# Causal attention in a two-block fp32 kernel: values as the stationary operand, two heads in two column halves, and the inverse sums turned by TensorE

## The reference, cut to what matters

```python
def one_block(args):                      # Q_BLOCK = 128 queries
    q_blk, blk_idx = args
    s = jnp.einsum('bhqd,bhkd->bhqk', q_blk, k).astype(jnp.float32) * scale
    query_pos = blk_idx * Q_BLOCK + jnp.arange(Q_BLOCK)
    s = jnp.where(key_pos[None, :] <= query_pos[:, None], s, NEG_INF)
    p = jax.nn.softmax(s, axis=-1).astype(v.dtype)
    return jnp.einsum('bhqk,bhkd->bhqd', p, v)
...
o = o.transpose(0, 2, 1, 3).reshape(bsz, seq, N_HEADS * V_DIM)
x = x + o @ mla_w_o[j]
```

## Time and profile before

| | |
|---|---|
| median of 3 runs | 1814.56 us (1811.64 to 1814.99) |
| the profiled execution | 1814.82 us, its span 1813.0 us |
| TensorE matmuls busy | 1755.1 us, 97% |
| VectorE / ScalarE / GpSimd busy | 817.3 / 665.4 / 705.8 us |
| mean granted clock of TensorE | 0.985 of full speed |

### The profile page before, as it was taken

How to read it: one execution, slowest core, us unless ns; L and a number is a source line. 1 busy time by engine, 2 the same in 40 slices (tenths; PEclk the granted TensorE clock), 3 DMA queues, 4 the chain that set the end, 5 groups by cost and what they waited for, 6 DMA issues and landing times.

```text
span 1813.0 us, 22687 instructions
## 1 busy us (share of the span) xinstructions
PE 1755.1 (97%) x9006; PEld 1459.8 (81%) x9006; DVE 817.3 (45%) x1398; ACT 665.4 (37%) x1128; POOL 705.8 (39%) x331
## 2 busy tenths in 40 slices
PE   8999999999999887999999999999999999999999
PEld 6887877787788676789888888888888888888887
DVE  4876999679866536414211111147665311111111
ACT  3332334143243555524322322266755333122221
POOL 5422334435444222243453444424711244344442
PEclk9999999999999898899999999999999999999999
DMA  9422324443535447322333233222200333332332
GB/s 243 100 70 82 86 78 143 124 140 117 167 109 165 134 158 239 105 93 82 100 98 93 88 105 99 81 82 74 75 1 13 93 94 93 94 104 85 101 95 80
DMA packets 242280, 189.61 MB, mean 105 GB/s; under 512 B 41472, under 2 KB 199296, under 8 KB 242176
## 3 DMA queue, kind: packets, MB, share of 16 engines
q1 hardware_dynamic: 238176, 180.33, 33.3%
q10 hardware_dynamic: 4000, 7.84, 1.3%
HBM read 168.74 MB, written 19.40 MB: 104 GB/s over the span
## 4 chain that ended last, share of the span: by engine, by line
PE 82%; DVE 11%; ACT 4%; issue 2%; DMA 1%; ACTq 1%; POOL 0%; DVEq 0%; SPq 0%
PE ps L371 12%; PE ps L373 12%; PE ps L372 12%; PE ps L397 9%; PE ps L398 9%; PE ps L399 9%; PE ps L428 3%; PE ps L429 3%; PE ps L430 3%; PE ps L881 2%; PE ps L862 2%; PE ps L872 1%; ACT w_hi L1147 1%; DVE x_rows L1669 1%; PE ps L854 1%
## 5 line engine op out<-in xcount | busy, mean ns | idle before, releaser
L1020 POOL TENSOR_TENSOR w_lo<-w_raw,w_hi 128x1024 fp32r<-128x1024 f32 (+3 forms) x283 | 668.6, 2373 | 1033.0 <-ACT w_hi L1147 1033.0
L371 PE MATMUL ps<-a_hi,w_hi 128*128 128x512 f32 (+1 forms) x1184 | 442.4, 374 | 4.3 <-POOL w_lo L1020 4.3
L373 PE MATMUL ps<-a_hi,w_lo 128*128 128x512 f32 (+1 forms) x1184 | 440.4, 372 | 0.0
L372 PE MATMUL ps<-a_lo,w_hi 128*128 128x512 f32 (+1 forms) x1184 | 440.3, 372 | 0.0
L1147 ACT ACTIVATE w_hi<-w_raw 128x1024 fp32r<-128x1024 f32 (+3 forms) x283 | 284.9, 1018 | 213.1 <-DMA w_raw<-in_ffn_w_gate_up_dram 70.9
L371 PEld LDWEIGHTS ps<-a_hi,w_hi 128*128 128x128 f32 x1184 | 223.0, 188 | 45.4 <-issue 7.2
L373 PEld LDWEIGHTS ps<-a_hi,w_lo 128*128 128x128 f32 x1184 | 223.0, 188 | 38.9
L372 PEld LDWEIGHTS ps<-a_lo,w_hi 128*128 128x128 f32 x1184 | 223.1, 188 | 38.1
L2134 DVE TENSOR_TENSOR ev<-ps,xh 128x512 f32<-128x512 f32 x44 | 30.4, 692 | 411.9 <-PE ps L373 383.0
L397 PE MATMUL ps<-w_hi,h_hi 128*128 128x512 f32 x476 | 190.7, 401 | 7.2 <-DVE x_rows L1641 3.4
L398 PE MATMUL ps<-w_lo,h_hi 128*128 128x512 f32 x476 | 189.5, 398 | 0.0
(11 more groups left out here) (346 smaller groups left out, 2395.6 us busy)
## 6 DMA issues: line engine op xcount, KB each, us to landing
w_raw<-in_ffn_w_gate_up_dram SPq DMA_DIRECT2D x88, 512.0 KB, 3.8
w_raw<-in_w_up_dram SPq DMA_DIRECT2D x44, 512.0 KB, 3.8
w_raw<-in_ffn_w_down_dram SPq DMA_DIRECT2D x40, 512.0 KB, 3.6
w_raw<-in_w_in_dram SPq DMA_DIRECT2D x20, 512.0 KB, 4.3
w_raw<-in_w_down_dram SPq DMA_DIRECT2D x20, 512.0 KB, 4.2
s_records<-stage SPq DMA_DIRECT2D x16, 544.0 KB, 5.3
w_raw<-in_ssm_w_glu_dram SPq DMA_DIRECT2D x16, 512.0 KB, 3.6
rec<-s_records SPq DMA_DIRECT2D x12, 544.0 KB, 3.7
```

The lines of the kernel that those rows point to most:

```text
L371: pe.matmul(bank, wh, xh_, start=first, stop=False)
L372: pe.matmul(bank, wh, xl_, start=False, stop=False)
L373: return pe.matmul(bank, wl, xh_, start=False, stop=last)
L1020: pool.tensor_tensor(w_lo[:, n % RING, 0:w], w_raw[:, n % RING, 0:w], w_hi[:, n % RING, 0:w].bitcast(F), ALU.subtract).then_inc(lo_made, 1)
```

## The change

- The values become the stationary operand (64 columns), the turned probabilities move. Tile layout: `p_ts` holds two heads, so that for key block j all queries from block j on lie in one row of 512, 384, 256 or 128 numbers.
- `head_out` goes; `pair_out(n)` makes the output of heads 2n and 2n + 1, one in partitions 0 to 63 and one in 64 to 127 of one bank, the heads alternating. The output comes out turned, with queries along the row. It is issued in the even loop turns from h = 2 on, behind the scores of t = 1; that of the last pair lies inside the first product with `mla_w_o_2`.
- The inverse sums are wanted as a row of the same layout. VectorE takes the reciprocal of the 8 columns of sums of a pair, each repeated 64 times (`inverse_sums`, output 128 x 512), in odd loop turns behind `masked(h + 1, 0)`. TensorE waits for it (`sum_inverse`) and turns it with 4 transposes (`inverses`), ScalarE copies it to `inv_rows`, VectorE multiplies the pair's output by it in PSUM (`pair_scaled`), and ScalarE and VectorE split the product into `a_hi` and `a_lo`.
- `head_turn(h + 2)` moves from the end of the loop turn to t = 1.
- `turn_rows("o_t", ...)` and its wait go.

```diff
-            def head_out(h):
-                b = open_bank(("o", h))
+            def inverses(n):
+
+                pe.wait_ge(sum_inverse, n + 1)
+                b = open_bank(("inv", n))
                 for t in range(TT):
...
+                    m = pe.transpose(b[:, t * P:t * P + P], inv_b[:, t, :, :].rearrange("p i e -> p (i e)"),
+                                     ident[:, :])
+                close_bank(("inv", n), m)
+
+            def pair_out(n):
+
+                b = split_bank(("o_t", n))
+                for i in range(2):
+                    for t in range(TT):
+                        pe.wait_ge(*freed[bank_no[("pt", 2 * n + i, t)]])
+                for j in range(TT):
+                    for i in range(2):
+                        m = pe.matmul(b[VD * i:VD * i + VD, j * P:SEQ], v_n[:, j, 2 * n + i, :],
+                                      p_ts[i][:, :, :].rearrange("p a c -> p (a c)")[:, j * SEQ:j * SEQ + SEQ - j * P],
+                                      start=(j == 0), stop=(j == TT - 1))
+                close_bank(("o_t", n), m)
...
             for h in range(NH):
                 for t in range(TT):
                     if h + 1 < NH:
                         head_scores(h + 1, t)
+                    if t == 1 and h >= 2 and h % 2 == 0:
+                        pair_out(h // 2 - 1)
                     head_probs(h, t)
-                if h + 2 < NH:
-                    head_turn(h + 2)
-                head_out(h)
-            pe.wait_ge(*freed[bank_no[("o", NH - 1)]])
-            turn_rows("o_t", lambda t, k: o_n[:, t, k * P:k * P + P], KT)
-            by_tile = turned_tiles()
-            rows_product(("w_o", 0), mla_w_o_2[0], h_hi, h_lo, KT, 0, HALF, 2, wait_t=by_tile)
+                    if t == 1 and h % 2:
+                        inverses(h // 2)
+                    if t == 1 and h + 2 < NH:
+                        head_turn(h + 2)
+            rows_product(("w_o", 0), mla_w_o_2[0], a_hi, a_lo, KT, 0, HALF, 2, wait_k=lambda k: pair_split + k + 1,
+                         inside=lambda n: pair_out(NH // 2 - 1) if n == 0 else None)
...
             for h in range(NH):
-                for t in range(TT):
+                for t in range(2):
                     if h + 1 < NH:
                         exponentials(h + 1, t)
...
+                if h % 2:
+                    release(("inv", h // 2), act.activation(inv_rows, full(act, ("inv", h // 2)), ACT.Copy))
                 if h + 2 < NH:
                     q_turned(h + 2)
+                if h >= 2 and h % 2 == 0:
+                    pair_rows(h // 2 - 1)
+                if h + 1 < NH:
+                    exponentials(h + 1, 2)
+                b = full(act, ("pt", h, TT - 1)).rearrange("p (j c) -> p j c", j=TT)
+                release(("pt", h, TT - 1), act.activation(turned_probs(h, TT - 1), b, ACT.Copy))
+                if h + 1 < NH:
+                    exponentials(h + 1, 3)
+            pair_rows(NH // 2 - 1)
...
+            def inverse_sums(n):
+
+                v.wait_ge(prob_ready, (2 * n + 2) * TT)
+                o = 16 + 8 * (n % 2)
+                sums = st[:, o:o + 8].rearrange("p (i t) -> p t i", i=2)
+                v.reciprocal(inv_b[:, :, :, :], sums.unsqueeze(3).to_broadcast([P, TT, 2, VD]))\
+                    .then_inc(sum_inverse, 1)
+
+            def pair_scaled(n):
+
+                b = full(v, ("o_t", n))
+                v.wait_ge(*freed[bank_no[("inv", n)]])
+                v.tensor_tensor(b, b, inv_rows, ALU.mult).then_inc(o_scaled, 1)
+
...
             for h in range(NH):
+                pair = h // 2 - 1 if h >= 2 and h % 2 == 0 else None
                 for t in range(TT):
                     if h + 1 < NH:
                         masked(h + 1, t)
...
+                    if t == 0:
+                        if h % 2:
+                            inverse_sums(h // 2)
+                        continue
+                    for tt in ((0, 1) if t == 1 else (t,)):
+                        if pair is not None and tt == 0:
+                            v.wait_ge(*closed(("o_t", pair)))
+                        if tt < TT - 1:
+                            b = full(v, ("pt", h, tt))[:, 0:(tt + 1) * P].rearrange("p (j c) -> p j c", j=tt + 1)
+                            release(("pt", h, tt), v.tensor_copy(turned_probs(h, tt), b))
+                        if pair is not None and tt == 0:
+                            pair_scaled(pair)
+                    if t == 1:
+                        if h + 2 < NH:
+                            k_turned(h + 2)
+                        if pair is not None:
+                            split(("o_t", pair), *row_split(a_hi, a_lo, pair))
+            pair_scaled(NH // 2 - 1)
+            split(("o_t", NH // 2 - 1), *row_split(a_hi, a_lo, NH // 2 - 1))
```

More of the change, by code:

```diff
@@ L112, in program @@
         w_hi = fixed("w_hi", [P, RING, CW], R)
+        xh_at = at_now[0]
         xh = fixed("xh", [P, 2, D], F)
@@ L198, in program @@
         sq = xh[:, 0, 0:2 * HALF].rearrange("p (a c) -> p a c", a=2)
-        nrm = xh[:, 1, 0:9 * HC * TT * HN].rearrange("p (a b c e) -> p a b c e", a=3, b=3, c=HC)
+        inv_rows = ev[:, 1, :]
+        nrm = scratch("nrm", [P, 3, 3, HC, TT * HN], F, 89.5)
         rot = scratch("rot", [P, 2, NH, ROPE // 2], F, 81)
-        o_n = nc.alloc_sbuf_tensor_at("o_n", [P, TT, NH * VD], F, offset=base + 32 * KB)
         qk_t = scratch("qk_t", [QK, 2, 2, SEQ], F, 64)
@@ L205, in program @@
         prob = scratch("prob", [P, 2, TRI], F, 72)
-        p_t = scratch("p_t", [P, TRI], F, 82)
-        q_rot = scratch("q_rot", [P, 2, 2, TT, HN, ROPE // 2], F, 87)
-        q_trig = scratch("q_trig", [P, 4, TT, ROPE // 2], F, 91)
+        p_ts = [scratch("p_t0", [P, TT + 1, 3 * P], F, 82),
+                nc.alloc_sbuf_tensor_at("p_t1", [P, TT + 1, 3 * P], F, offset=xh_at)]
+        q_rot = ev[:, :, :].rearrange("p b (a t h e) -> p b a t h e", a=2, t=TT, h=HN)
+        q_trig = scratch("q_trig", [P, 4, TT, ROPE // 2], F, 96.25)
+        inv_b = scratch("inv_b", [P, TT, 2, VD], F, 94)
         hg = scratch("hg", [P, 2 * ROPE], F, 94)
@@ L274, in program @@
         prob_ready = sem("prob_ready")
+        sum_inverse = sem("sum_inverse")
+        o_scaled = sem("o_scaled")
         x_in = [sem(f"x_in{i}") for i in range(KT // XC)]
@@ L892, in _ @@
                               ready=lambda t: pe.wait_ge(cq_ready, t + 1), through_ev=True)
+            pair_split = n_split[0]
             for t in range(TT):
@@ L898, in _ @@
                         head_scores(h + 1, t)
+                    if t == 1 and h >= 2 and h % 2 == 0:
+                        pair_out(h // 2 - 1)
                     head_probs(h, t)
-                if h + 2 < NH:
-                    head_turn(h + 2)
-                head_out(h)
-            pe.wait_ge(*freed[bank_no[("o", NH - 1)]])
-            turn_rows("o_t", lambda t, k: o_n[:, t, k * P:k * P + P], KT)
-            by_tile = turned_tiles()
-            rows_product(("w_o", 0), mla_w_o_2[0], h_hi, h_lo, KT, 0, HALF, 2, wait_t=by_tile)
+                    if t == 1 and h % 2:
[4 more added lines that the diff above has]
+                         inside=lambda n: pair_out(NH // 2 - 1) if n == 0 else None)
             ffn1 = xh_turner("ffn1")
-            rows_by_tile(("w_o", 1), mla_w_o_2[0], h_hi, h_lo, KT, HALF, HALF, 2, after=turn_two(ffn1[0]))
+            rows_by_tile(("w_o", 1), mla_w_o_2[0], a_hi, a_lo, KT, HALF, HALF, 2, after=turn_two(ffn1[0]))
             ffn("f3", ffn_w_gate_up_2[1], ffn_w_down_2[1], (0, FF), ffn1)
@@ L963, in row_split, with turned_probs @@
             return lambda e: e, hi[:, k, :], lo[:, k, :]
+        def turned_probs(h, t):
+            return p_ts[h % 2][:, 0:t + 1, t * P:t * P + P] if t < TT - 1 else p_ts[h % 2][:, 1:TT + 1, 0:P]
         def inverse(a, c, e):
@@ L1477, in exponentials @@
                                scale=-1.0, bias=st[:, 8 * (h % 2) + t:8 * (h % 2) + t + 1],
-                               accum_out=st[:, 16 + 8 * (h % 2) + t:17 + 8 * (h % 2) + t]).then_inc(prob_ready, 1)
+                               accum_out=st[:, 16 + TT * (h % 4) + t:17 + TT * (h % 4) + t]).then_inc(prob_ready, 1)
             for n, (q, c) in enumerate(LATENT_ORDER):
@@ L1511, in _, with pair_rows @@
                 exponentials(0, t)
+            def pair_rows(n):
+                act.wait_ge(o_scaled, n + 1)
+                split(("o_t", n), *row_split(a_hi, a_lo, n))
             for h in range(NH):
-                for t in range(TT):
+                for t in range(2):
                     if h + 1 < NH:
                         exponentials(h + 1, t)
[L1516 to L1519, removed]
+                if h % 2:
+                    release(("inv", h // 2), act.activation(inv_rows, full(act, ("inv", h // 2)), ACT.Copy))
                 if h + 2 < NH:
                     q_turned(h + 2)
-            act.wait_ge(*closed(("o", NH - 1)))
```

(3 more changed lines are left out.)

## The result

The changed kernel takes 1841.92 us (median of 4 runs, 1841.42 to 1844.29) against 1813.13 of the kernel before on the same chips; the ratio is 1.0166, 95% interval 1.0151 to 1.0181. It is slower, by some 29 us. The forecast was 1861 with a range of 1835 to 1880: the side and the mechanism were right, the likely value 19 us too high.

A forecast was written before the change was run, and what follows sets the result against it. TensorE was taken to bound the attention, 103.6 us. Less work but new stalls made it 125.8, so +22.2; with 24 us for the lowered clock, 1814.8 + 22.2 + 24 = 1861 us, range 1835 to 1880.

The forecast's parts named there:

- TensorE bounds the attention, and work alone would win 16.1 us.: Attention: TensorE has no idle time, VectorE and ScalarE hide; less TensorE work wins 16.1 us if no wait is added.
- The halves overlap.: Pair's output on TensorE: two column halves run beside each other, 2.56 us a pair, bounds 2.13 and 4.27.
- The reciprocal takes 3.42 us.: VectorE's 128 x 512 reciprocal: 6.4 ns a column from three narrower widths, 3.42 us, lower bound 0.69.
- TensorE waits for it, 38.6 us in all.: Odd turns: TensorE stands for the inverse sums, 4.0 us first, 6 x 4.8, 5.8 last; 38.6 us.
- The clock falls behind each stall, 24 us.: After each of 8 stalls the clock halves for 6.0 us of work, losing 3.0 us; 24 us, bounds 8 x 1.7 and 8 x 4.1.
- The sum.: Attention's terms: 63.2 kept steps, 3.5 inverses, 20.5 outputs, 38.6 stalls; 125.8 us at full clock, plus 24 for the clock.
- The end goes, GpSimd and ScalarE hide their part.: Attention's end, 4.8 us, is removed; GpSimd's head groups and ScalarE's added 1.2 us a pair cost nothing.
- A clock that stays full: Rival: the attention's stalls come, but activity on either side keeps the clock full; 1837 us, chance 0.13.
- serial halves: Rival: the column halves of a pair's output don't overlap, 13.7 us more; 1875 us, chance 0.10.
- a short reciprocal: Rival: VectorE's reciprocal is priced like an ordinary operation, 0.69 us, stalls sum to 16.7; 1815 us, chance 0.08.
- The last rival: Rival: VectorE hides more, the exponential comes earlier, stall about 3.3 us with a short clock fall; 1839 us, chance 0.07.
- the 2.2 us that I had read from one trace: TensorE's clock: it fell to 0.50 around all nine idle times of 2.2 us and more; 1.99 and 1.74 passed.

The follow-up runs named there:

- the run with serial halves: Changed kernel with the 16 matmul passes of a pair's output issued head after head instead of alternating; 1856.65 us, 1.0248 to the kernel before.
- both edits: Changed kernel with VectorE inverting 8 columns then copying them out, and TensorE's wait and four transposes at the odd turn's end; 1801.17 us, 0.9936 to the kernel before.
- the narrow variant: Changed kernel with VectorE inverting only a pair's 8 columns of sums, then copying them out to 128 x 512; 1813.09 us, 1.0004 to the kernel before.
- the kernel with both edits and serial halves: Kernel with both edits, its output passes issued head after head instead of alternating; 1810.96 us, 1.0002 to the kernel before.

## Why the prediction was right, and where it was off

- *TensorE bounds the attention, and work alone would win 16.1 us.* Right in kind: with the waits gone the kernel is 11 us faster, and its attention 12.9. Not 16, since a pair still takes 11.68 us there and not the 11.38 of the terms (12.74 - 4.36 + 0.44 + 2.56), with 0.29 us of waiting for ScalarE in each, and since the last head waits twice for its exponentials (0.67 and 0.63).
- *The halves overlap.* Right; 2.30 us a pair in the place of 2.56. Ahead of the first pass lies a gap of 0.17 (score 1 ends its issue at 1358.42, the output starts at 1358.59) whose cause no run separates; with it the output takes 2.47. So the value from stepping through the passes was 0.09 too high with the gap; the passes alone lay nearer the lower bound, 2.13.
- *The reciprocal takes 3.42 us.* 3.352. The line through three widths held at 8 times the widest of them. That its slope agrees with a repeat count of 8 is loosely said: 6.3 ns a column is 6 times the 1.04 ns of a plain copy of line 2265 before (287 ns for 128 columns, 552 for 384), not 8 times.
- *TensorE waits for it, 38.6 us in all.* Right in kind, a little too much: 3.9 for the first, 6 x 4.26, 5.4 for the last (from the end of what was issued to the inverses), 34.8. The reciprocal began 1.90 us into the odd turn instead of 2.3, since the output ahead of it in the chain was shorter.
- *The clock falls behind each stall, 24 us.* This term was mis-sized. It fell all 8 times, but stayed low for 3.1 to 3.6 us of work, not 6.0. In rows: the inverses, turning and score 2 took 3.50 us (1352.52 to 1356.02) instead of 0.44 + 0.87 + 0.65 = 1.96; 7 x 1.54 and 1.7 at the last are 12.5 us, and the run in which TensorE was kept busy gives 13.2. The mean of six other places was a poor guide; its lower bound, 8 x 1.7 = 13.6, is nearly what came. Of the 19 us by which 1861 was too high, 16.8 lie in the attention (63.2 + 3.5 + 20.5 + 38.6 + 24 = 149.8 forecast, 133.0 measured), 11.5 of them in this term and 3.8 in the waits; the earlier start of the attention is most of the rest.
- *The sum.* 63.2 + 3.5 + 8 x 2.47 + 34.8 + 12.5 = 133.8 us against 133.0 measured.
- *The end goes, GpSimd and ScalarE hide their part.* Right in the changed kernel; the kernels with the narrow reciprocal meet GpSimd in a way that the trace of before does not show (below).
- *The rivals.* A clock that stays full would have been near in time (1837) and is refuted by the windows; serial halves and a short reciprocal fell with their rows. The last rival, 1839, is nearest in time: its short fall of the clock came, its stall of 3.3 us did not (34.8/8 = 4.35). The time alone could not have told these apart; the rows do.

## What to carry to other kernels

Price an operation by its width on its engine before moving data into a convenient shape: inverting 8 numbers and spreading them costs a fifth of spreading and inverting 512. When an engine must wait for a new result, look at what stands behind the wait and behind the producer, and put both where the queues have slack; here that was worth 35 us with the long instruction kept. And these stalls of 4 to 5 us on TensorE were paid again in the clock afterwards, here a third as much on top (12.5 on 34.8).

## What the runs showed of the hardware beyond that

How long the clock stays low is no property of the idle time. In the run with serial halves six stalls have the same 4.15 us of idle time; the low stretches around their ends are 6.83 us long four times and 3.41 twice, here one of each:

```profile
1320.15:1326.98 6.83, 5.06 (x18) 4.08 (x19) 4.22 (x9) 2.11 (x5) 2.12 (x1) 0.50 0.00 0
1361.11:1364.52 3.41, 2.96 (x13) 2.88 (x14) 1.35 (x6) 1.84 (x4) 0.00 (x0) 0.50 0.00 0
```

Nor did the fall keep to the 2.2 us that I had read from one trace, on either side of it. Below it, an idle time of 1.99 us passed at full clock in the kernel before; the same one, 1.98 or 1.99, was followed by a low stretch in the changed kernel (from 1205.42 for 3.41 us) and in three more of the nine traces. With only TensorE's wait moved, one of six stalls of 1.90 was followed by one, and so was the idle time of 1.74 ahead of the attention (from 1291.32), which passed in the eight others. With the wide reciprocal moved, a low stretch begins at 1389.0, at the end of three idle times of 0.78, 0.73 and 0.64 that lie within 3.1 us. Above it, idle times of 2.26 and 2.25 (303 and 746 us, only TensorE's wait moved) and of 2.29 (303 us, both edits) passed at full clock. Every idle time of 2.56 us and more between matmuls, in all nine traces, has a low stretch at it or right behind it. What decides in between I can't tell from these runs.

In the narrow variant one copy of the reciprocals, SBUF to SBUF, took 2.42 us instead of 0.43. It began while GpSimd had just started on a weight chunk:

```profile
1310.47 4.84 POOL L1043 TENSOR_TENSOR w_lo<-w_raw,w_hi 128x1024 fp32r<-128x1024 f32 x2
1310.67 2.42 DVE L2295 COPY inv_b<-st 128x512 f32<-128x512 f32 x1
```

It ended (1313.09) soon after the first of these two GpSimd instructions (half of 4.84, 1312.89), and TensorE stood 3.45 us, the longer of the two stalls named above. The same copy in the kernel with both edits and serial halves, and with both edits:

```profile
1309.46 4.85 POOL L1043 TENSOR_TENSOR w_lo<-w_raw,w_hi 128x1024 fp32r<-128x1024 f32 x2
1309.91 2.18 DVE L2295 COPY inv_b<-st 128x512 f32<-128x512 f32 x1
```

```profile
1310.42 0.43 DVE L2295 COPY inv_b<-st 128x512 f32<-128x512 f32 x1
1310.46 1.29 POOL L1025 TENSOR_TENSOR q_n<-q_n,nrm 128x512 f32<-128x512 f32 x1
```

In the first the copy again began behind a GpSimd instruction and ended (1312.09) just after half of its 4.85 (1311.88). In the second the copy began first and kept its 0.43, and it was GpSimd's instruction that took 1.29 us instead of the 1.05 of its others. The six last copies of each kernel, with GpSimd idle beside them, take 0.43. The Trainium skill, "SBUF — State Buffer", section SBUF: two separate sides, describes this as a port pair that VectorE and GpSimd take exclusively for a whole instruction. These rows fit it, with either engine first; no run was made to vary it.
